# Recurrence heads as a pipeline, norms by ScalarE, side units moved to the sparse attention

## The reference

```python
h = rms_norm(x, attn_norm[l])
(aq, ak, av, iq, ik, iw, bq, bf, bi, bg, cq, ckv, ckpe, gate_logits) = jnp.split(h @ w_in[l], split_pts, axis=-1)
o_a = dsa_attention(...)          # sparse: 4 heads over the keys that an indexer chose
o_b = hgrn2_mixer(bq, bf, bi, bg, ...)   # gated linear recurrence, 4 heads of 128 x 128
q_c = rms_norm(cq, mla_q_norm[l]) @ mla_w_qb[l]      # latent queries, cq of 384 columns
kv_c = rms_norm(ckv, mla_kv_norm[l]) @ mla_w_kvb[l]  # latent keys and values, 256 columns
o_c = mla_attention(...)          # 4 heads, causal, rope on 64 columns
mixed = g_a * (o_a @ w_up_a[l]) + g_b * (o_b @ w_up_b[l]) + g_c * (o_c @ w_up_c[l])
```

## Time and profile before

| | us |
|---|---|
| runs | 1572.63, 1574.62, 1575.78 (median 1574.62) |
| span of the profiled execution, first to last instruction | 1571.3 |
| TensorE busy, share of the span | 1421.7, 90% |
| VectorE busy | 965.8, 61% |
| ScalarE busy | 525.4, 33% |
| GpSimd busy | 52.7, 3% |

### The profile page before, as it was taken

How to read it: one execution, slowest core, us unless ns; L and a number is a source line. 1 busy time by engine, 2 the same in 40 slices (tenths; PEclk the granted TensorE clock), 3 DMA queues, 4 the chain that set the end, 5 groups by cost and what they waited for, 6 DMA issues and landing times.

```text
span 1571.3 us, 18872 instructions
## 1 busy us (share of the span) xinstructions
PE 1421.7 (90%) x7109; PEld 1103.0 (70%) x7110; DVE 965.8 (61%) x1621; ACT 525.4 (33%) x840; POOL 52.7 (3%) x43
## 2 busy tenths in 40 slices
PE   5998888896989878799899999999799999988898
PEld 4758788785567655688688888888659955565676
DVE  6249767676166677775535555633397648568772
ACT  5247332231322563323433423432223211213421
POOL 0000000001000260000000000000000002000000
PEclk9999999997989989899899999999999999999999
DMA  5212111121222111443134443232422122430001
GB/s 227 75 48 87 67 41 54 55 84 61 87 108 81 48 42 35 151 177 127 56 132 155 167 181 146 69 111 77 152 67 83 54 79 68 154 129 1 1 1 54
DMA packets 40170, 141.04 MB, mean 90 GB/s; under 512 B 13072, under 2 KB 17552, under 8 KB 27536
## 3 DMA queue, kind: packets, MB, share of 16 engines
q1 hardware_dynamic: 34896, 131.05, 23.8%
q10 hardware_dynamic: 5184, 8.78, 1.6%
HBM read 128.94 MB, written 8.39 MB: 87 GB/s over the span
## 4 chain that ended last, share of the span: by engine, by line
PE 53%; DVE 5%; issue 1%; ACT 1%; DVEq 0%; ACTq 0%
PE turn L714 24%; PE score L699 7%; PE score L714 7%; PE sum L699 5%; PE sum L714 2%; PE sum L1284 1%; PE sum L1166 1%; PE score L1166 1%; DVE stat L2597 1%; DVE probs L1825 1%; PE score L1258 1%; PE turn L836 1%; PE turn L1270 1%; DVE probsT L1825 1%; PE turn L1137 0%
## 5 line engine op out<-in xcount | busy, mean ns | idle before, releaser
L1867 DVE TENSOR_TENSOR ring_r<-ring,heads_r 128x1024 fp32r<-128x1024 f32 (+3 forms) x161 | 186.1, 1156 | 228.7 <-ACT heads_r L1392 193.0
L1392 ACT ACTIVATE heads_r<-ring 128x1024 fp32r<-128x1024 f32 (+3 forms) x161 | 161.8, 1005 | 250.5 <-DMA ring<-wstream 129.6
L714 PE MATMUL score<-h_sb_r,heads_r 128*128 128x512 f32 x408 | 164.4, 403 | 0.0
L714 PE MATMUL turn<-tiles_r,heads_r 128*128 128x512 f32 x368 | 144.6, 393 | 0.0
L714 PE MATMUL turn<-h_sb_r,heads_r 128*128 128x512 f32 x336 | 132.1, 393 | 8.1 <-DVE ring_r L1867 8.1
L714 PE MATMUL turn<-wide_r,heads_r 128*128 128x512 f32 x312 | 121.8, 391 | 0.0
L714 PE MATMUL turn<-wide_r,ring_r 128*128 128x512 f32 x312 | 121.6, 390 | 0.0
L714 PE MATMUL score<-x_sb_r,heads_r 128*128 128x512 f32 x256 | 110.1, 430 | 8.9 <-DVE ring_r L1867 6.5
L714 PE MATMUL score<-x_sb_r,ring_r 128*128 128x512 f32 x256 | 103.7, 405 | 0.0
L714 PEld LDWEIGHTS score<-h_sb_r,heads_r 128*128 128x128 f32 x408 | 79.9, 196 | 15.0 <-issue 0.2
L714 PEld LDWEIGHTS turn<-tiles_r,heads_r 128*128 128x128 f32 x368 | 70.1, 190 | 14.5
(11 more groups left out here) (398 smaller groups left out, 2925.8 us busy)
## 6 DMA issues: line engine op xcount, KB each, us to landing
ring<-wstream SPq DMA_DIRECT2D x95, 1024.0 KB, 4.9
ring<-wstream SPq DMA_DIRECT2D x16, 704.0 KB, 4.3
ring<-gated SPq DMA_DIRECT2D x6, 1024.0 KB, 7.2
gated<-tiles ACTq DMA_DIRECT2D x15, 256.0 KB, 2.0
gated<-probs ACTq DMA_DIRECT2D x9, 256.0 KB, 2.0
x_sb<-xT SPq DMA_DIRECT2D x4, 512.0 KB, 5.5
x_sb<-xT ACTq DMA_DIRECT2D x1, 2048.0 KB, 8.1
outT<-x_sb SPq DMA_DIRECT2D x1, 2048.0 KB, 6.3
```

The costliest lines, as they stand in the source:

```text
L714: return pe.matmul(out, a, w, **k) if moving else pe.matmul(out, w, a, **k)
L1392: step(act.activation(head_piece(p), chunk(name)[:, c:c + cols], ACT.Identity), f"head {p}")
L1867: step(dve.tensor_tensor(out, a, b, op), name)
```

## The change

The four places `tail` are gone, and eight places `dsa` stand behind `bias`. So 8 half units leave the stretch after the recurrence; every later gate moves up by four tiles, the latents' places now hold gates 5 to 7, and gates 20 to 23 are done beside the sparse attention, one half at every second item. The eight-part form moves with it from gates 21 to 23 to gates 17 to 19, the ones now at `bias`.

ScalarE takes the squares of `cq` and `ckv` right behind their drains and of each head's output from the bank `sum`, with the sum as a second output; GpSimd raises four groups of four means and one of eight. VectorE writes `REC_O` already normed at level 4 of the next head. The arguments of head h+1's two exponentials are made at level 5 of head h, the exponentials follow its last level's, and the operands between chunks follow the last masked copy. The latents are scaled by ScalarE during head 3, and their turns stand right behind head 3's products. The turns `rec o` move behind the `qb` products, and sine and cosine (table load, Sin, Abs, Sin) from behind ScalarE's last drain of the latents to the place behind the drains of `qbp`.

```diff
--- before.py
+++ after.py
@@ -134,8 +134,8 @@
-         [(f"tail {i}", 2) for i in range(4)] + [("latent 0", 2), ("latent 1", 4)] + [(f"mla {i}", 1) for i in range(18)] + \
-         [(f"bias {i}", 1) for i in range(6)]
+         [("latent 0", 2), ("latent 1", 4)] + [(f"mla {i}", 1) for i in range(18)] + [(f"bias {i}", 1) for i in range(6)] + \
+         [(f"dsa {i}", 1) for i in range(8)]
@@ -743,7 +743,7 @@
-                        for mm in split_tile(b[:, :], f"{tag}_{i}", e * KD * P, acts, None, "each" if tag == "gate" and 2 * i + e >= 21 else True):
+                        for mm in split_tile(b[:, :], f"{tag}_{i}", e * KD * P, acts, None, "each" if tag == "gate" and 17 <= 2 * i + e < 20 else True):
@@ -960,16 +960,11 @@
-            for i in range(4):
-                beside(f"tail {i}")
-            for n in range(NT):
-                turn(f"rec o {n}", [(REC_O[:, n, j * P:(j + 1) * P], P, j * P) for j in range(4)], (dve_step, at("rec normed")))
...
-                turn(f"cq {j}", [(CQ[:, n, j * P:(j + 1) * P], P, n * P) for n in range(NT)], (dve_step, at("latents normed")))
+                turn(f"cq {j}", [(CQ[:, n, j * P:(j + 1) * P], P, n * P) for n in range(NT)], (act_step, at("latents normed")))
...
@@ -978,6 +973,8 @@
+            for n in range(NT):
+                turn(f"rec o {n}", [(REC_O[:, n, j * P:(j + 1) * P], P, j * P) for j in range(4)], (sum_done, at("rec o out 3")))
@@ -1030,7 +1027,8 @@
-                      lambda h, j: ROW[:, j, 0:128], P, masked=lambda n: chosen[:, upto(n):upto(n + 1)])
+                      lambda h, j: ROW[:, j, 0:128], P, masked=lambda n: chosen[:, upto(n):upto(n + 1)],
+                      beside=lambda i: i < 16 and i % 2 == 0 and beside(f"dsa {i // 2}"))
@@ -1471,7 +1469,12 @@
-            EARLY = units_before(PLACE["latent 0"]) - 5 * NT - len(PROJ1G) - len(PROJ1C)
+            EARLY = units_before(PLACE["latent 1"]) - 5 * NT - len(PROJ1G) - len(PROJ1C)
...
@@ -1487,13 +1490,16 @@
+                    mean_square(stat[:, 52 + n:53 + n], CKV[:, n, :], SPARE[:, 0:256])
...
-                    drain(CQ[:, n, 256:384], "have cq" if n == NT - 1 else None, cols=128)
+                    drain(CQ[:, n, 256:384], cols=128)
+                    step(act.activation(SPARE, CQ[:, n, :], ACT.Square, scale=384 ** -0.5, accum_out=stat[:, 48 + n:49 + n]),
+                         "squared latents" if n == NT - 1 else None)
@@ -1522,18 +1528,43 @@
+            def rec_ends(h):
+                act.wait_ge(dve_step, at(f"rec args {h}"))
+                step(act.activation(REC_E[1], REC_E[1], ACT.Exp))
+                if h:
+                    act.wait_ge(dve_step, at(f"rec scaled {h - 1} {LEVELS - 1}"))
+                step(act.activation(REC_E[0], TL[:, 5 + h, :], ACT.Exp), f"rec ends {h}")
+            def rec_squares(h):
+                act.wait_ge(sum_full, at(f"full rec o {h}"))
+                for n in range(NT):
+                    step(act.activation(trig[:, 0:P], O[0][:, n * P:(n + 1) * P], ACT.Square, scale=P ** -0.5,
+                                        accum_out=stat[:, 32 + 4 * n + h:33 + 4 * n + h]), f"squared rec {h}" if n == NT - 1 else None)
+            def latent_normed(i):
+                v, n = (CQ, CKV)[i // NT], i % NT
+                if i == 0:
+                    act.wait_ge(pool_step, at("rstd latents"))
+                step(act.activation(v[:, n, :], v[:, n, :], ACT.Identity, scale=stat[:, 48 + i:49 + i]), "latents normed" if i == 7 else None)
+            rec_ends(0)
...
-                bt = TL[:, 5 + h, :]
-                act.wait_ge(dve_step, at(f"rec args {h}"))
-                step(act.activation(REC_E[0], bt, ACT.Exp), f"rec eb {h}")
-                step(act.activation(REC_E[1], REC_E[1], ACT.Exp), f"rec el {h}")
...
+                    if l == LEVELS - 1 and h < 3:
+                        rec_ends(h + 1)
...
-            for i in range(4):
-                beside(f"tail {i}")
+                    if l == 0 and h:
+                        rec_squares(h - 1)
+                    if h == 3:
+                        latent_normed(l)
+            latent_normed(7)
+            rec_squares(3)
@@ -1575,8 +1606,9 @@
+            drains(units_before(PLACE["dsa 0"]))
+            attention_exp("dsa", 4, lambda i, cols: LOGITS[i % 2][:, 0:cols], lambda i: i % 2 == 0 and beside(f"dsa {i // 2}"))
...
-            attention_exp("dsa", 4, lambda i, cols: LOGITS[i % 2][:, 0:cols])
@@ -1967,22 +1999,42 @@
...
+            def rec_cross(h):
+                dve.wait_ge(act_step, at(f"rec ends {h}"))
+                tt(REC_QX, TL[:, 9 + h, :], REC_E[0], ALU.mult)
+                tt(REC_KX, TL[:, h, :], REC_E[1], ALU.mult)
...
-                step(dve.memset(REC_AT, 0.0))
-                lev = con("level").rearrange("p (l t) -> p l t", l=LEVELS + 1)
+            def rec_mean(h):
+                r = stat[:, 32 + h:48:4]
+                dve.wait_ge(act_step, at(f"squared rec {h}"))
+                ts(r, r, EPS, None, ALU.add, name=f"mean rec {h}")
+            def rec_normed(h):
+                dve.wait_ge(pool_step, at(f"rstd rec {h}"))
+                step(dve.tensor_tensor(REC_O[:, :, h * P:(h + 1) * P], O[0][:, :].rearrange("p (c t) -> p c t", c=4),
+                                       stat[:, 32 + h:48:4].unsqueeze(2).broadcast_to([P, 4, P]), ALU.mult),
+                     f"rec o out {h}", sum_done)
+            rec_end_args(0)
+            beside("rank 7")
+            rec_cross(0)
@@ -2004,6 +2056,9 @@
+                if h:
+                    dve.wait_ge(sum_full, at(f"full rec o {h - 1}"))
+                step(dve.memset(REC_AT, 0.0))
@@ -2017,48 +2072,30 @@
+                    if l == LEVELS - 2 and h < 3:
+                        rec_end_args(h + 1)
...
+                    if h and l == 2:
+                        rec_mean(h - 1)
+                    if (h, l) == (2, 5):
+                        dve.wait_ge(act_step, at("squared latents"))
+                        ts(stat[:, 48:56], stat[:, 48:56], EPS, None, ALU.add, name="mean latents")
...
+                    if h and l == 4:
+                        rec_normed(h - 1)
...
-                dve.wait_ge(sum_full, at(f"full rec o {h}"))
-                step(dve.tensor_copy(REC_O[:, :, h * P:(h + 1) * P], O[0][:, :].rearrange("p (c t) -> p c t", c=4)),
-                     None, sum_done)
-            o16, w0 = part(wide, 2560, 2048, k=16), work[:, 0:4 * T]
-            tt(w0, part(wide, 2560, 2048), part(wide, 2560, 2048), ALU.mult)
-            r16 = stat[:, 32:48]
-            beside("tail 0")
-            step(dve.tensor_reduce(r16, w0.rearrange("p (k t) -> p k t", k=16), AX.X, ALU.add))
-            step(dve.tensor_scalar(r16, r16, 1.0 / 128, EPS, ALU.mult, ALU.add), "mean rec")
-            for i in range(1, 4):
-                beside(f"tail {i}")
-            dve.wait_ge(pool_step, at("rstd rec"))
-            tt(o16, o16, r16.unsqueeze(2).broadcast_to([P, 16, P]), ALU.mult, "rec normed")
...
-            dve.wait_ge(gemm_done, at("have cq"))
-            for name, v, wd, c0 in (("cq", CQ, 384, 48), ("ckv", CKV, 256, 52)):
-                sq = part(work, 2560, 4 * wd, k=NT)
-                tt(sq, v, v, ALU.mult)
-                step(dve.tensor_reduce(stat[:, c0:c0 + 4], sq, AX.X, ALU.add))
-                small_rstd(name, stat[:, c0:c0 + 4], wd)
-                for n in range(NT):
-                    ts(v[:, n, :], v[:, n, :], stat[:, c0 + n:c0 + n + 1], None, ALU.mult,
-                       name="latents normed" if (name, n) == ("ckv", NT - 1) else None)
+                if h < 3:
+                    rec_cross(h + 1)
...
-            beside("latent 0")
+            weight_rests(upto=pieces_through(PLACE["latent 0"]))
+            rec_mean(3)
@@ -2069,6 +2106,14 @@
+            rec_normed(3)
+            weight_rests(upto=pieces_through(PLACE["latent 1"]))
...
@@ -2085,7 +2130,6 @@
-            beside("latent 1")
@@ -2159,7 +2203,8 @@
-            attention_max("dsa", 4, probs_over_sums("dsa", lambda n: work[:, 0:T], 4), o_to_tiles("dsa", 13), biased)
+            attention_max("dsa", 4, probs_over_sums("dsa", lambda n: work[:, 0:T], 4), o_to_tiles("dsa", 13), biased,
+                          beside=lambda i: i < 16 and i % 2 == 0 and beside(f"dsa {i // 2}"))
```

45 lines of the change are left out of this document (23 added, 22 removed).

## The result

| | before | after |
|---|---|---|
| runs, median (lowest to highest) | 1575.05 (1572.63 to 1575.78), 4 runs | 1535.14 (1533.13 to 1538.73), 4 runs |
| span of the profiled execution | 1571.3 | 1535.2 |
| TensorE busy | 1421.7 | 1412.6 |
| VectorE, ScalarE busy | 965.8, 525.4 | 949.7, 540.5 |

The changed kernel takes 0.9745 of the time before (95% interval 0.9725 to 0.9764), 39.9 us less. 1529.8 was forecast, with a range of 1518 to 1547: the time lies in it, 5.3 us above the forecast. The same kernel measured again later, beside two experiments, gave 1538.09 and a ratio of 0.9758 (0.9737 to 0.9780).

What follows compares the result with a forecast made beforehand. TensorE, busy 90% of the span, was taken as the bound, through its waits and low clock. Terms -21.0 - 42.2 - 3.0 + 1.1 + 20.3 = -44.8 gave 1526.5 us, plus 3.3 to the median: 1529.8; range 1518 to 1547.

Steps and rivals of the forecast that it cites:

- The heads, -21.0: Heads 1 to 3: operands ready before each first block save 5.7, 7.65 and 7.65 us; bounds 13 to 24.
- Rival 1: Heads 1 to 3: VectorE sets the pace, 36.5 us a head, gain 13 instead of 21, 1538 us; chance 0.13.
- what is late next: Head starts: the far block, needing the first masked copy and the cleared weights, is late by 0.3 to 0.6 us.
- Each wait costs twice: TensorE's long waits at head starts and before turns: the idle time, then a stretch at granted clock 0.50 (1.2 GHz).
- Head 3 to the latent attention, -42.2: From head 3's products to the latent attention: 97.5 us becomes 55.3; 21.6 of the gain only moved elsewhere.
- rival 3: Behind head 3: latents scaled too late between ScalarE's Exps, TensorE waits some 5 us, 1535 us; chance 0.05.
- The start of the latent attention, -3.0: Latent attention starts at full clock instead of 0.50, saving 3.0 us; bounds 0 and 4.
- The gates' weight rests and ScalarE's heads keep their lead of one place: Head 3 to the latent attention: side units' weights are still prepared one place ahead; no time of its own given.
- Sparse attention, +20.3: Eight added halves make the sparse attention 58.6 us instead of 38.3; bounds +15 and +27.
- Rival 2: Sparse attention takes the halves in full, lengthening its latency chain: +27 instead of 20, 1537 us; chance 0.12.
- Squares load no table: ScalarE's added Squares run in the table loaded for Exp: 0 us of loads, against 64 us estimated by the skill page.
- Rival 5: Heads 1 to 3: small waits at many levels pull the clock to 0.50 throughout, 1623 us, slower; chance 0.03.

Runs made afterwards that it cites:

- heads_serial: Changed kernel with head h+1's exponentials, arguments and operands again at its start, VectorE not waiting for head h's output products: 1529.5 us, ratio 0.9736.
- heads_serial_filled: Changed kernel with next-head operands made only after the output products, TensorE's wait filled with 20 overwritten products: 1546.86 us, ratio 0.9830.
- rest_ahead: Changed kernel, but VectorE makes the weight rest of the latent attention's first side unit ahead, behind the rotation: 1530.99 us, ratio 0.9733.

## Why the prediction was right, point by point

- **The heads, -21.0.** Measured -20.7, with 33.59 and 33.48 us for heads 2 and 3 (33.2 forecast) and 34.06 for head 1 (34.4). In head 1 there is one wait of 0.62 us (at 242.92) instead of three with 1.5 in all. The forecast's own terms give 33.2 + 1.5 = 34.7 for it, and so a gain of 5.4 from its 40.13 and not 5.7; the smaller remainder made up for that slip. Heads 2 and 3 each have one wait of 0.46 us, where 0.32 were counted; the rest of the 0.3 above 33.2 stays open. Rival 1 (VectorE sets the pace) is out: the heads are 33.5 us apart and not 36.5, with TensorE busy 33.0 of them and VectorE 27.4. The step on "what is late next" was right. The reading that the operands had to be made while TensorE does the output products was right too, but a smaller edit reaches it: `heads_serial` shows that the exponentials could have stayed where they were.
- **Each wait costs twice.** Right as to the mechanism. The low clock costs 2.75 us in heads 2 and 3 by `heads_serial_filled`, and 0.5 in head 1; the expectation of that run, 3 to 3.5 in each, was too high.
- **Head 3 to the latent attention, -42.2.** Measured -42.5, and not by terms that cancel: turns 3.5 us (3.6 forecast), `latent 0` 5.6 (5.4), `qb` 10.3, `rec o` 2.8 (3.0), `qbp` 5.2, `kvb` and `latent 1` 24.7 (24.8), the last turns 3.0. The longest wait is 0.85 us, at the first score. The latents were scaled in time: rival 3 is out. The rotation had 11.5 us to spare, 10 forecast.
- **The start of the latent attention, -3.0: wrong.** The stage is 0.2 us longer. The failed step is the sentence "The gates' weight rests and ScalarE's heads keep their lead of one place". VectorE's call that made the rests through one place beyond `latent 1` became one that goes through `latent 1` alone, so the rest of the first half in the latent attention fell behind the first maximum: 1.80 us of waiting and 1.6 of low clock behind it (the first two scores are 7.10 us apart, and 3.72 in `rest_ahead`). With that rest in place the stage is 1.7 us shorter than before (94.96), so the forecast would still have been 1.3 us too high; the wait of 1.88 us for VectorE's copy stands there.
- **Bias, +1.1.** +0.6 in the first profile, +2.2 in the second: a stage that varies by more than the term.
- **Sparse attention, +20.3.** Measured +20.9, with 59.2 us, TensorE busy 52.6 of them, and 8.14 behind it, as forecast (58.6 and 8). Rival 2 would have been +27.
- **Squares load no table.** Right; the row taken from elsewhere in the program carried over. The Trainium skill's page "ScalarE: Activation LUTs" (Table sets: the hidden batching unit) does not name Square in its short list of what every set holds. The prediction read that as two loads at each group, 64 us; the page doesn't say so, and the trace shows none.
- **The clock in the heads.** Rival 5 is out: 1.00 through them. But the small waits at many levels that it started from did not come either (one of 0.46 us in heads 2 and 3, one of 0.62 in head 1), so these runs don't show what many such waits would do to the clock.
- **The unchanged code, 0.** It took 4.0 us more, at a lower clock (mean 0.96, before 0.97), with TensorE busy 4.5 us longer in the same instructions. The start varies as well: 189.95 to 191.66 us in the profiles of the later kernels, before 189.98. Together with the start (+1.3) that is 5.3 of the 8.7 us by which the profiled span (1535.2) is above the 1526.5 worked out for it; the latent attention is 3.2 of it. No step of the prediction allowed for the unchanged nine hundred microseconds to move. The 3.3 us from span to median were not there either: the median is 1535.14. In each run whose span is known the time is 1.7 to 1.8 us above it, and the rest hangs on which execution was profiled: the profiled one of the changed kernel took 1537.01 us, 1.9 above the median. That the median is only 5.3 us above the forecast, where the profile is 8.7 above the sum, is luck.

## What to carry to other kernels

When a long wait stands at the head of a loop, look first at what the engine that is waited for is itself waiting for: here VectorE's wait for a result that it didn't need for the next operands was 18.6 of 20.3 us, and the start one level earlier 1.7. Moving side work from a place without waits to another that has few is worth little: 0.9 us by stages for eight halves. When side work is moved, follow the lead of each of the engines that prepare it, call by call; a lead of one place lost in a rewritten call costs a wait at the next place where that engine is late. And when work that makes a wait shorter is moved to its front, count the whole chain behind: the 8 us behind the sparse attention came back as 5 us two products later.

## What the runs showed of the hardware

TensorE's granted clock fell in or right behind stretches in which TensorE is busy by the profile all the time: with products of a single column (x49, 7.81 us at 0.66 in one kernel, 5.27 at 1.00 in another). Behind them it was 0.52 and 0.51 for the full-size products, over 5.1 and 3.5 us. Runs of the same program differed by 14 us in 1530, the shortest with a mean clock of 0.970 and the longest with 0.956; where profiles of the same code differed by 4.0 and by 12.6 us, TensorE's busy time in the same instructions did by 4.5 and 12.3. Twenty small products in a wait of 4 us kept the clock at 1.00 and paid 2.75 us back in two heads, 0.5 in a third.
